# Low part of the weights: subtracted by VectorE at fixed points of its program, or by GpSimd in a loop of its own

## What is computed

```python
u = rms_norm(x, norm_mix_w);  proj = u @ w_in
# HGRN2: f = lb + (1-lb)*sigmoid(hf);  q = silu(hq), k = 1-f, v = hi, log_g = log(f)
# GLA:   log_g = log_sigmoid(glr @ gla_gate_w2 + gla_gate_b) / 16;  q, k, v from proj
S_t = diag(exp(log_g_t)) @ S_{t-1} + outer(k_t, v_t);   o_t = scale * (q_t @ S_t)
y = concat(rms_norm(o_h) * silu(z_h), rms_norm(o_g) * silu(z_g)) @ w_out
h = x + y
e = rms_norm(p @ ple_proj, ple_norm_w)
gate = sigmoid(rms_norm(h, ple_gate_norm_w) @ ple_gate_w + ple_gate_b)
out = rms_norm(h + gate * e, final_norm_w)
```

## Time and profile before

| what | value |
|---|---|
| runs of the kernel before | 2405.06, 2406.80, 2407.32 us (median 2406.8) |
| the profiled execution: its own time | 2405.83 us |
| its span in the trace | 2404.0 us |
| mean granted TensorE clock, share of full | 0.986 |
| TensorE, matmuls: busy | 2266.9 us (94%) |
| VectorE busy | 1432.9 us (60%) |
| ScalarE busy | 1003.6 us (42%) |
| GpSimd busy | 892.3 us (37%) |
| DMA moved | 234.13 MB, mean 97 GB/s |

### The profile page before, as it was taken

One profiled execution on the slowest core, in us unless ns is written; L12 is line 12 of the kernel. 1 busy time (PEld: TensorE's weight loads), 2 busy tenths in 40 slices (PEclk: granted clock), 3 DMA queues, 4 the chain that ended last, 5 costly groups with the idle time before them and its releaser, 6 DMA issues.

```text
span 2404.0 us, 31946 instructions
## 1 busy us (share of the span) xinstructions
PE 2266.9 (94%) x10652; PEld 1869.4 (78%) x10652; DVE 1432.9 (60%) x2555; ACT 1003.6 (42%) x1738; POOL 892.3 (37%) x364
## 2 busy tenths in 40 slices
PE   6999999999999899999889999999999998999995
PEld 5878888888887688878678888887888876887884
DVE  5566666645545732466776666666445567225886
ACT  5444444433343622345444444444333345224443
POOL 2433333333333245344433333334333323544441
PEclk9999999999999899999999999999999999999997
DMA  4222222222221333344332222222222214333333
GB/s 166 88 70 85 72 70 83 74 88 70 87 84 66 130 127 116 106 175 131 105 123 88 70 86 71 87 70 82 77 87 70 88 66 149 122 118 98 121 115 112
DMA packets 72832, 234.13 MB, mean 97 GB/s; under 512 B 8352, under 2 KB 8608, under 8 KB 71872
## 3 DMA queue, kind: packets, MB, share of 16 engines
q1 hardware_dynamic: 72768, 233.28, 29.2%
HBM read 216.47 MB, written 16.78 MB: 97 GB/s over the span
## 4 chain that ended last, share of the span: by engine, by line
issue 67%; POOL 24%; PE 7%; DVE 1%; POOLq 1%; ACT 0%; DVEq 0%
POOL w_lo L407 24%; PE acc L415 2%; PE acc L416 2%; PE acc L417 2%; DVE feat L1268 0%; POOLq L403 0%; POOLq L406 0%; PE ms L581 0%; POOLq L407 0%; DVE work L1247 0%; DVE work L1070 0%; DVE sq_sum L1076 0%; DVE work L1072 0%; DVE work L1082 0%; DVE work L1233 0%
## 5 line engine op out<-in xcount | busy, mean ns | idle before, releaser
L407 POOL TENSOR_TENSOR w_lo<-w_raw,w_hi 128x1024 fp32r<-128x1024 f32 x360 | 892.1, 2499 | 1469.5 <-ACT w_hi L685 1469.4
L415 PE MATMUL acc<-act_hi,w_lo 128*128 128x512 f32 x2880 | 1161.8, 403 | 30.5 <-ACT work L951 13.0
L416 PE MATMUL acc<-act_lo,w_hi 128*128 128x512 f32 x2880 | 1126.9, 391 | 0.0
L417 PE MATMUL acc<-act_hi,w_hi 128*128 128x512 f32 x2880 | 1126.9, 391 | 0.0
L415 PEld LDWEIGHTS acc<-act_hi,w_lo 128*128 128x128 f32 x2880 | 544.6, 189 | 149.5 <-issue 25.1
L417 PEld LDWEIGHTS acc<-act_hi,w_hi 128*128 128x128 f32 x2880 | 543.3, 189 | 116.3
L416 PEld LDWEIGHTS acc<-act_lo,w_hi 128*128 128x128 f32 x2880 | 545.1, 189 | 103.1 <-issue 1.2
L685 ACT CAST w_hi<-w_raw 128x1024 fp32r<-128x1024 f32 x360 | 361.7, 1046 | 490.6 <-PE acc L417 444.0
L730 ACT ACTIVATE work<-work 128x512 f32<-128x512 f32 x168 | 106.0, 631 | 347.4 <-DVE work L1102 347.4
L1108 DVE TENSOR_TENSOR work<-work 128x256 f32<-128x256 f32 x168 | 101.7, 605 | 136.9 <-ACT work L730 136.7
L487 PEld LDWEIGHTS lv<-work 128*128 128x128 f32 x672 | 99.4, 191 | 57.0 <-DVE work L1109 45.8
(11 more groups left out here) (169 smaller groups left out, 1718.2 us busy)
## 6 DMA issues: line engine op xcount, KB each, us to landing
w_raw<-in_slabs SPq DMA_DIRECT2D x360, 512.0 KB, 3.4
e_scratch<-work SPq DMA_DIRECT2D x32, 256.0 KB, 2.0
work<-in_x_feat SPq DMA_DIRECT2D x32, 256.0 KB, 2.6
work<-e_scratch SPq DMA_DIRECT2D x32, 256.0 KB, 2.6
out<-feat SPq DMA_DIRECT2D x32, 256.0 KB, 2.5
work<-in_x SPq DMA_DIRECT2D x7, 1024.0 KB, 5.0
work<-in_x SPq DMA_DIRECT2D x2, 512.0 KB, 10.3
work<-in_p SPq DMA_DIRECT2D x2, 512.0 KB, 3.7
```

The source lines that it names most:

```text
L407: nc.gpsimd.tensor_tensor(w_lo[par][:, j, :], w_raw[j][:, :], w_hi[par][:, j, :].bitcast(F32), ALU.subtract).then_inc(w_lo_ready, 1)
L415: nc.tensor.matmul(ps, lhs_lo, rhs_hi, start=start, stop=False)
L416: nc.tensor.matmul(ps, lhs_hi, rhs_lo, start=False, stop=False)
L417: return nc.tensor.matmul(ps, lhs_hi, rhs_hi, start=False, stop=stop)
```

## The change

GpSimd's loop is taken out. A function `low_weights(h, s, par, js)` in VectorE's program waits for the cast and does the same subtraction with the same operands; it is called at fixed points, for slab s of half h:

```diff
-            with pool.Fori(0, HALVES * SLABS // 2) as i:
-                for par in range(2):
-                    for j in range(2):
-                        pool.wait_ge(w_hi_ready, i * 4 + (2 * par + j + 1))
-                        nc.gpsimd.tensor_tensor(w_lo[par][:, j, :], w_raw[j][:, :],
-                                                w_hi[par][:, j, :].bitcast(F32), ALU.subtract
-                                                ).then_inc(w_lo_ready, 1)
...
+            def low_weights(h, s, par, js=(0, 1)):
+
+                for j in js:
+                    vec_e.wait_ge(w_hi_ready, (h * SLABS + s) * 2 + (j + 1))
+                    v.tensor_tensor(w_lo[par][:, j, :], w_raw[j][:, :], w_hi[par][:, j, :].bitcast(F32),
+                                    ALU.subtract).then_inc(w_lo_ready, 1)
...
                 log_sigmoid(h, c + 3 * HEADS, g_t)
+                if more_slabs:
+                    low_weights(h, c + (G_SLAB + 2), par)
                 vec_e.wait_ge(sig_ready, h * SIGMOIDS + (c + (3 * NH + 2 * NG + 1)))
...
                 level_mul(R, 0)
+                low_weights(h, next_slab, 1)
                 log_sigmoid(h, z_no, acc[1][:, :])
...
                 state_chain(R, 1, state_h[:, bass.ds((n - 1) * P, P)])
+                low_weights(h, s + 2, 0)
                 for l in range(LEVELS - 2):
                     next_level(R, l)
+                low_weights(h, s + 3, 1)
                 vec_e.wait_ge(hv_ready, r0 + 1)
                 f_gate(h, n)
                 mask_level(R, LEVELS - 2)
                 decay_sum(h, n)
                 mask_level(R, LEVELS - 1)
+                low_weights(h, s + 4, 0)
                 o_copy(R, 1)
...
+                low_weights(h, s + 2, 0)
                 for l in range(LEVELS - 2):
+                    if l == LEVELS - 3:
+                        low_weights(h, s + 3, 1)
                     next_level(R, l)
...
                 for l in (LEVELS - 2, LEVELS - 1):
                     mask_level(R, l)
 
+                low_weights(h, s + 4, 0)
...
                 o_copy(R, rec_nb)
+                low_weights(h, s + 5, 1)
                 o_norm(R, rec_nb)
...
                     next_level(r0, 0)
+                low_weights(h, s + 6, 0)
+                if last:
                     next_level(r0, 1)
                 log_sigmoid(h, sg + 1, acc[0][:, :])
...
+            low_weights(0, 0, 0)
             st.fresh()
             for h in range(HALVES):
...
+                low_weights(h, 1, 1)
                 if h:
                     g_first(h - 1, KT // 2 - 1, 1)
                     g_rest(h - 1, KT // 2 - 1, 1)
...
+                    if e in (2, 3):
+                        low_weights(h, I_SLABS + 1, 1, (e - 2,))
+                    if e in (10, 11):
+                        low_weights(h, O_SLAB, 0, (e - 10,))
...
+                low_weights(h, O_SLAB + 1, 1)
                 row_factors(h * 2 + 1, r_e[:, :])
...
                     v.tensor_tensor(sq_sum[:, :], sq_sum[:, :], (t1, t2)[par], ALU.add).then_inc(h_added, 1)
+                    if more_slabs:
+                        low_weights(h, c + (O_SLAB + 2), par)
...
+                low_weights(h, G_SLAB + 1, 1)
                 row_factors(h * 2 + 2, r_h[:, :])
```

22 lines of the change are left out of this document (13 added, 9 removed).

## The result

The changed kernel takes **2334.5 us** in the median (2333.9 to 2336.2, four runs) against 2407.1 us for the kernel before on the same chip (2405.1 to 2408.9): a ratio of 0.970 with a 95% interval of 0.9683 to 0.9717, 72.5 us less. The prediction was 2343 us with a range from 2328 to 2364. The profiled execution took 2333.9 us, its span is 2332.1 us, against 2404.0 before, and the granted clock 0.990 against 0.986.

What follows compares the result with a forecast made beforehand. The kernel can only get shorter where TensorE waits, mostly for VectorE instructions blocked by GpSimd's subtractions. Terms summing to 63.5 us take the profiled 2405.8 to 2342.3; the median, 1.0 above, is forecast at 2343 us, range 2328 to 2364.

Steps and rivals of the forecast that it cites:

- What bounds the kernel, and what the subtraction blocks: Whole kernel: only TensorE's waits can shrink; GpSimd's subtraction pairs cost VectorE up to 4.9 us in one piece.
- The price on VectorE: One 128x1024 subtraction on VectorE: 1.23 us, 2.3 us for a slab's two.
- HGRN, 33.9: 14 HGRN iterations: waits for level 6 and the readout, 1.05 us each, go; gain 33.9 us.
- GLA heads, 9.8: Eight GLA heads: one wait each at level 5 goes, less a charge at level 6; gain 9.8 us.
- The charge of 0.2 us for level 6: GLA heads: the pair for s+3 ahead of level 6 makes it ready at 576.4 for an ask at 576.2.
- The last GLA head, -0.9: Last GLA head, both halves: the pair delays level 3, then the state update's copy, and level 4 by 0.45 us; loss 0.9.
- Embedding stage, 8.0: Embedding stage, both halves: pairs on GpSimd no longer block VectorE's running sum; gain 2 x 4.0 us.
- the replay: Embedding stage retraced with moved subtractions: readout 1.4 us earlier, 1.7 at the bank, about 0.9 at the next two.
- Gate stage and end of half 0, 9.3: Gate stage through the turn of the halves: blocked VectorE instructions shorten, 9.4 us earlier; -0.1 at the turn.
- The rival on TensorE's clock: Shorter gaps spare three or four low-clock stretches at 2 to 3 us: 2334 us; chance 0.07.
- weight ring: Gate stage: load-to-next-load ring of 11.7 us costs some 24 tiles 0.8 each, 2362 us; chance 0.15 with used-up slack.
- slower: A VectorE subtraction at GpSimd's 2.4 us makes gate tiles, GLA heads and HGRN late: 2441 us; chance 0.06.

Runs made afterwards that it cites:

- the spare work on GpSimd: Changed kernel plus a subtraction on GpSimd after each of the 360 casts, its result unused: 2522.9 us.
- Moving the pair: Changed kernel with the last GLA head's subtraction pair for slab s+6 put behind next_level(r0, 1) instead of ahead of it: 2328.4 us.
- the run with the mask first: On the 2317.2 us kernel, embedding stage: a subtraction and one low part of y moved behind the mask of level 6: 2316.3 us.
- level 4 first: On the 2328.4 us kernel, last GLA head: next_level(r0, 2) put ahead of four low parts of y: 2326.2 us.

## Why the prediction was right, and where it was off

- **What bounds the kernel, and what the subtraction blocks.** Right. The waits named are the ones that went, and the spare work on GpSimd brought the blocking back. One detail was wrong: I wrote that VectorE's instructions with both inputs in SBUF stand still. Also those with one input in SBUF did (L1245, 2.07 in place of 0.49 us; the copy, 2.30 in place of 0.16); those that read a PSUM bank did not (L1082 at 65.59, 0.69 us). And the exponential of level 6 follows VectorE's argument, by 0.66 us, and not the casts, as I had it; with 3.3 us to spare it made no difference.
- **The price on VectorE.** 1.23 us predicted, 1.219 measured, a pair 2.36 against 2.3. The Trainium skill's rule in "VectorE: DVE Perf Modes", section "The DRAIN you can't avoid", by which the next instruction starts only when the pipe is empty and a pair would take 2.46, is not what these rows show: the second starts 0.08 us ahead of the first one's end. The same section adds that an instruction which is not held starts earlier; that fits.
- **HGRN, 33.9 against 37.5.** The mechanism and both slacks held (3.3 and 0.8 us against 3.0 and 0.6). The mis-sized term is the price of a wait: I took 1.05 us and 0.15 of refill, and the slabs became 1.34 us shorter each. A wait of 1.06 us is counted from the recorded end of the product before it, which took 0.39 us; products in a row start 0.225 us apart, so the wait moves the next start by 1.06 + 0.39 - 0.23 = 1.22 us. With a wait ahead, the four matmuls of a level also take 0.71 us in place of 0.60, which makes some 1.33.
- **GLA heads, 9.8 against 13.1.** The charge of 0.2 us for level 6 was not found (0.1 at most), and a fifth place per half was missing from the sum, so it is ten places of 1.31 us and not eight of 1.23: in the last head's fifth slab an output transposition and level 0 waited 0.32 and 1.55 us, and now 0 and 0.77.
- **The last GLA head, -0.9 against -2.8.** The chain was named rightly, through the exponential to the copy to the state update, with a wait of 1.8 us (1.55 measured). The step that failed is what follows, "level 4 comes 0.45 later than now": the wait ahead of the state update pushed TensorE back by 1.7, but the wait at level 4 hardly fell, from 3.53 to 3.34 us in half 0, and rose to 3.70 in half 1. That it is because the silu stands behind the same copy on ScalarE is an argument, not shown. Moving the pair gave 2.3 us per half back.
- **Embedding stage, 8.0 against 6.8.** The wait of 2.73 us for a bank became 0.9, but the readout did not come 1.4 us earlier as the replay had it: it waits 1.97 and 2.06 us, about as before the change (1.84 and 2.17), because mask 6 stands behind a subtraction and a low part of y (the run with the mask first brought it to 0.6).
- **Gate stage and end of half 0, 9.3 against 13.1.** The largest miss, and mis-sized, not misplaced: giving the stage back to GpSimd cost 12.3 us. The two tiles that also scale rows took 12.4 and 13.7 us on VectorE, and now 11.5 each (from one L1231 to the next), and the six slabs ahead of the last, 11.0 to 12.6 us long, are 10.88 now. What the sum lacked is the rest: TensorE's waits of 3.04 and 6.39 us became 0 and 1.6, in place of "below 1" and "about 4", and the granted clock had been 0.50 from 1202.0 to 1208.8 us, around the first product of half 1.

The clock in 12 us around the first products of half 1, before and after (window, busy us and instructions of each engine, granted clock):

```profile
1198.00:1210.00 12.00, 5.61 (x23) 4.20 (x22) 7.80 (x13) 7.28 (x13) 0.00 (x0) 0.72 0.13 44
...
1158.00:1170.00 12.00, 10.40 (x66) 8.50 (x63) 10.30 (x17) 7.16 (x12) 0.00 (x0) 1.00 0.25 87
```

0.72 on average before and 1.00 after. The rival on TensorE's clock expected three or four such stretches fewer, and its mechanism did come, beside the forecast's: ahead of the last 24 us, where both kernels end at the lower level, the clock stands at 0.50 in eight stretches before (41 us together) and in five after (20 us). The measured 2334.5 us is also that rival's number (2334), but that is in part chance: of the 8.3 us beyond the forecast 6.9 come from the HGRN iterations and the GLA heads, where the granted clock is 1.00 in both traces. What the three stretches were worth was not measured by itself; it lies within the terms of the last GLA head, the embedding stage and the gate stage. The **weight ring** rival did not come: from the fourth to the fifteenth every gate slab of both halves takes 10.88 us, none lost 0.8. The **slower** rival was rightly held improbable by the price, and its size was wrong (2441 stated, 2566 with a price of 2.4). The gate stage was priced about rightly there (61 us, measured 57), the GLA heads (20 against 46) and the HGRN iterations (17 against 92) far too low: it let only half of the gain go there, while level 2 and the readout became late by more than had been gained.

## What to carry to other kernels

Before judging an idle helper engine as free, look at what the others' instructions last beside it: the places where GpSimd held up VectorE's short instructions (0.42 us that took 2.4) cost this kernel 72 us more than 424 us of work given to VectorE. When work moves from an engine that runs it on arrival to one with a fixed order, its price is set by the place: put it behind the last instruction that somebody waits for, and count both its own time and its wait for its input; one place ahead of a mask cost over 43 us. And after each removed wait look for the next one in the same chain, as more than half of such a gain came back elsewhere with level 4 first, and most of it with the mask first.
